# Gate/up and down products: high weights times both halves of the activations in one 512-column matmul

## What is computed

```python
hn2 = rmsnorm(x, norm2_w[l])
gu = hn2 @ w_gate_up[l]                                   # 2048 x (2 * 5632)
x = x + (jax.nn.silu(gu[..., :FFN_HIDDEN]) * gu[..., FFN_HIDDEN:]) @ w_down[l]   # 5632 x 2048
return rmsnorm(x, norm_f_w)
```

## Time and profile before

| | before |
|---|---|
| median of the runs | 2630.93 us |
| span of the profiled execution | 2631.7 us |
| its mean granted TensorE clock | 0.996 |
| TensorE matmul busy | 2584.1 us (98%) |
| VectorE busy | 1587.5 us (60%) |
| ScalarE busy | 1207.2 us (46%) |
| DMA, mean | 169 GB/s |

### The profile page before, as it was taken

How to read it: one execution, slowest core, us unless ns; L and a number is a source line. 1 busy time by engine, 2 the same in 40 slices (tenths; PEclk the granted TensorE clock), 3 DMA queues, 4 the chain that set the end, 5 groups by cost and what they waited for, 6 DMA issues and landing times.

```text
span 2631.7 us, 53153 instructions
## 1 busy us (share of the span) xinstructions
PE 2584.1 (98%) x21314; PEld 2521.6 (96%) x21314; DVE 1587.5 (60%) x1984; ACT 1207.2 (46%) x1412; POOL 44.2 (2%) x48
## 2 busy tenths in 40 slices
PE   8999999999999999999999999999999999999997
PEld 8999999999999999999999997679999999999997
DVE  6445777665455566677755556886655555555544
ACT  5444456543357665443444444234544444444442
POOL 0000021000000000000000000000000000000000
PEclk9999999999999999999999999999999999999999
DMA  6554532455554434555565653235565656555563
GB/s 226 177 175 160 176 106 80 154 186 175 178 172 157 144 111 137 186 185 193 194 205 168 207 192 120 78 99 197 185 198 192 193 191 196 191 192 194 187 199 127
DMA packets 123706, 446.06 MB, mean 169 GB/s; under 512 B 13594, under 2 KB 15925, under 8 KB 123440
## 3 DMA queue, kind: packets, MB, share of 16 engines
q1 hardware_dynamic: 122208, 438.82, 50.6%
q0 software_dynamic: 1360, 5.27, 0.6%
HBM read 441.94 MB, written 2.10 MB: 169 GB/s over the span
## 4 chain that ended last, share of the span: by engine, by line
PE 90%; DVE 5%; ACT 3%; issue 1%; DMA 0%; POOL 0%; DVEq 0%; SPq 0%; ACTq 0%
PE PS L1885 25%; PE PS L1887 25%; PE PS L1886 25%; PE PS L1948 2%; PE PS L1949 2%; PE PS L1950 2%; PE PS L2299 1%; DVE lo L1057 1%; ACT hi L540 1%; PE PS L2251 1%; PE PS L2032 0%; PE PS L2048 0%; PE PS L2131 0%; PE PS L2108 0%; PE PS L2022 0%
## 5 line engine op out<-in xcount | busy, mean ns | idle before, releaser
L1885 PE MATMUL PS<-XH,hi 128*128 128x256 f32 (+1 forms) x5152 | 1449.4, 281 | 16.7 <-DVE lo L1051 11.6
L1887 PE MATMUL PS<-XH,lo 128*128 128x256 f32 (+1 forms) x5152 | 1445.5, 281 | 0.0
L1886 PE MATMUL PS<-XL,hi 128*128 128x256 f32 (+1 forms) x5152 | 1441.0, 280 | 0.0
L1051 DVE TENSOR_TENSOR lo<-raw,hi 128x1024 fp32r<-128x1024 f32 x704 | 852.7, 1224 | 750.7 <-ACT hi L535 747.2
L535 ACT ACTIVATE hi<-raw 128x1024 fp32r<-128x1024 f32 x704 | 740.3, 1059 | 944.6 <-PE PS L1887 915.5
L1885 PEld LDWEIGHTS PS<-XH,hi 128*128 128x128 f32 x5152 | 970.2, 188 | 21.4 <-issue 16.6
L1886 PEld LDWEIGHTS PS<-XL,hi 128*128 128x128 f32 x5152 | 972.5, 189 | 1.4 <-issue 1.2
L1887 PEld LDWEIGHTS PS<-XH,lo 128*128 128x128 f32 x5152 | 969.8, 188 | 0.0
L1948 PE MATMUL PS<-XH,hi 128*128 128x256 f32 (+1 forms) x768 | 229.2, 298 | 0.3 <-DVE XL L1122 0.3
L1950 PE MATMUL PS<-XH,lo 128*128 128x256 f32 (+1 forms) x768 | 216.0, 281 | 0.0
L1949 PE MATMUL PS<-XL,hi 128*128 128x256 f32 (+1 forms) x768 | 215.8, 281 | 0.0
(11 more groups left out here) (331 smaller groups left out, 1568.3 us busy)
## 6 DMA issues: line engine op xcount, KB each, us to landing
raw<-stream SPq DMA_DIRECT2D x828, 512.0 KB, 4.1
H<-h_in SPq DMA_DIRECT2D x4, 544.0 KB, 8.2
y_win<-windows POOLq DMA_DIRECT2D x2, 1024.0 KB, 6.4
out<-H SPq DMA_DIRECT2D x4, 512.0 KB, 3.8
w_t<-w POOLq DMA_DIRECT2D x2, 512.0 KB, 5.5
dftm<-dft POOLq DMA_DIRECT2D x1, 1024.0 KB, 8.1
ml_m<-mask_ml POOLq DMA_DIRECT2D x1, 512.0 KB, 3.9
a_m<-masks_a POOLq DMA_DIRECT2D x1, 272.0 KB, 6.4
```

Source lines behind the costliest of these rows:

```text
L1051: dve.tensor_tensor(halves(lo, s, q.tokens), raw_halves(s), halves(hi, s, q.tokens).bitcast(F32), ALU.subtract)\
L1885: pe.matmul(PS[:, bank, 0:n], w_hi, x_hi, start=start, stop=False)
L1886: pe.matmul(PS[:, bank, 0:n], w_hi, x_lo, start=False, stop=False)
L1887: return pe.matmul(PS[:, bank, 0:n], w_lo, x_hi, start=False, stop=stop)
```

## The change

XH and XL become the two planes of one tensor `XHL`, and GH and GL those of `GHL`. In gate/up and down, `wide_passes` replaces `passes`: one matmul of the hi weights with a 2 x 256 column access over both planes, written to all 512 columns of the bank, and one of the lo weights with the hi plane, added to columns 0 to 255. The second half of a bank then holds w_hi*x_lo. It is added at the read-out: VectorE gets, for gate and for up, a second scaled copy out of PSUM into `g_t` and an addition; for down a second addition to `H`. ScalarE's silu waits for that addition (`g_gate`), and its final squares for both (`down_added`). The other products keep `passes`.

```diff
-        x_hi_flat = sb(ctx, "XH", [P, NT * T + 4 * STEP], F32R)
-        x_lo_flat = sb(ctx, "XL", [P, NT * T + 4 * STEP], F32R)
+        x_flat = sb(ctx, "XHL", [P, 2, NT * T + 4 * STEP], F32R)
+        x_hi_flat, x_lo_flat = x_flat[:, 0, :], x_flat[:, 1, :]
...
-            g_hi_flat = sb(ph, "GH", [P, KICK + STEP + FT * SEQ], F32R)
-            g_lo_flat = sb(ph, "GL", [P, STEP + KICK + STEP + FT * SEQ], F32R)[:, STEP:]
+            g_flat = sb(ph, "GHL", [P, 2, KICK + 2 * STEP + FT * SEQ], F32R)
+            g_hi_flat, g_lo_flat = g_flat[:, 0, :], g_flat[:, 1, :]
             g_s = sb(ph, "g_s", [P, GROUP, SEQ])
             g_p = sb(ph, "g_p", [P, GROUP, SEQ])
+            g_t = sb(ph, "g_t", [P, GROUP, SEQ])
...
+        def x_both(both, k):
+
+            at = KICK + (STEP + k * SEQ if k else 0)
+            return both[:, :, at:at + SEQ]
...
-        def bank_group(gg, n):
-            return PS[:, 4 * gg:4 * gg + GROUP, 0:n]
+        def bank_group(gg, n, at=0):
+            return PS[:, 4 * gg:4 * gg + GROUP, at:at + n]
...
             def gate_up(p, gg):
                 if gg == 0:
-                    act.wait_ge(bank_free[0], p + (q.use0[0] + 2))
+                    act.wait_ge(S("g_gate"), p + 1)
                     act.activation(g_s[:, :, :], g_s[:, :, :], ACT.Silu).then_inc(S("g_silu"), 1)
...
             def final_squares(p, gg):
-                act.wait_ge(bank_free[gg], p + (prod["down"].use0[gg] + 2))
+                act.wait_ge(S("down_added"), 2 * p + gg + 1)
                 squares(2 * p + gg, f_sq, META, SEQ)
...
-            def residual(q, gain, scratch, tok0, n):
+            def residual(q, gain, scratch, tok0, n, wide=False):
 
                 def after(p, gg):
                     group_done(dve, q, p, gg)
                     dst = H[:, p * 8 + 4 * gg:p * 8 + 4 * gg + 4, T - q.tokens:T]
+                    if wide:
+                        own(dve.tensor_tensor(dst, dst, bank_group(gg, SEQ, SEQ), ALU.add))
                     dve.tensor_tensor(dst, dst, bank_group(gg, q.tokens), ALU.add).then_inc(bank_free[gg], 1)
                     dve.wait_ge(bank_free[gg], p + (q.use0[gg] + 2))
+                    if wide:
+                        dve.sem_inc(S("down_added"), 1)
...
             def gate_up(p, gg):
                 group_done(dve, q, p, gg)
                 if gg == 0:
-                    dve.tensor_tensor(g_s[:, :, :], bank_group(0, SEQ), rs, ALU.mult).then_inc(bank_free[0], 1)
+                    dve.tensor_tensor(g_s[:, :, :], bank_group(0, SEQ), rs, ALU.mult).then_inc(S("g_scaled"), 1)
+                    dve.tensor_tensor(g_t[:, :, :], bank_group(0, SEQ, SEQ), rs, ALU.mult).then_inc(bank_free[0], 1)
+                    dve.wait_ge(S("g_scaled"), 2 * p + 1)
+                    dve.wait_ge(bank_free[0], p + (q.use0[0] + 2))
+                    dve.tensor_tensor(g_s[:, :, :], g_s[:, :, :], g_t[:, :, :], ALU.add).then_inc(S("g_gate"), 1)
                 else:
-                    dve.tensor_tensor(g_p[:, :, :], bank_group(1, SEQ), rs, ALU.mult).then_inc(bank_free[1], 1)
+                    dve.tensor_tensor(g_p[:, :, :], bank_group(1, SEQ), rs, ALU.mult).then_inc(S("g_scaled"), 1)
+                    dve.tensor_tensor(g_t[:, :, :], bank_group(1, SEQ, SEQ), rs, ALU.mult).then_inc(bank_free[1], 1)
+                    dve.wait_ge(S("g_scaled"), 2 * p + 2)
                     dve.wait_ge(bank_free[1], p + (q.use0[1] + 2))
+                    dve.tensor_tensor(g_p[:, :, :], g_p[:, :, :], g_t[:, :, :], ALU.add).then_inc(S("g_up"), 1)
+                    dve.wait_ge(S("g_up"), p + 1)
                     dve.wait_ge(S("g_silu"), p + 1)
                     dve.tensor_tensor(g_p[:, :, :], g_s[:, :, :], g_p[:, :, :], ALU.mult).then_inc(S("g_prod"), 1)
...
-            follow(dve, prod["down"], chunk, tail_gu, [(2, residual(prod["down"], "norm_f", f_xg, META, SEQ))],
+            follow(dve, prod["down"], chunk, tail_gu, [(2, residual(prod["down"], "norm_f", f_xg, META, SEQ, True))],
...
+            def wide_passes(bank, w_hi, w_lo, both, k, start, stop):
+
+                x = x_both(both, k)
+                pe.matmul(PS[:, bank, :].rearrange("p (h t) -> p h t", h=2), w_hi, x, start=start, stop=False)
+                return pe.matmul(PS[:, bank, 0:SEQ], w_lo, x[:, 0, :], start=False, stop=stop)
...
+                                    if both is None:
+                                        ins = passes(4 * gg + j, q.tokens, w_hi, w_lo, x_tile(x_hi_flat, x, q.tokens),
+                                                     x_tile(x_lo_flat, x, q.tokens), *ends)
+                                    else:
+                                        ins = wide_passes(4 * gg + j, w_hi, w_lo, both, x, *ends)
...
-            product(prod["gate_up"], between={6: lambda: squares_sum(3, g_scratch, SEQ), 7: lambda: pe.wait_ge(S("rms_ready"), 4)})
-            product(prod["down"], g_hi_flat, g_lo_flat, pieces=("gl_ready", 0, 4))
+            product(prod["gate_up"], x_flat, between={6: lambda: squares_sum(3, g_scratch, SEQ), 7: lambda: pe.wait_ge(S("rms_ready"), 4)})
+            product(prod["down"], g_flat, pieces=("gl_ready", 0, 4))
```

More of the change, by code:

```diff
@@ L1887, in passes, with product @@
                 return pe.matmul(PS[:, bank, 0:n], w_lo, x_hi, start=False, stop=stop)
-            def product(q, xh=x_hi_flat, xl=x_lo_flat, between={}, pieces=None):
+            def wide_passes(bank, w_hi, w_lo, both, k, start, stop):
+                x = x_both(both, k)
+                pe.matmul(PS[:, bank, :].rearrange("p (h t) -> p h t", h=2), w_hi, x, start=start, stop=False)
+                return pe.matmul(PS[:, bank, 0:SEQ], w_lo, x[:, 0, :], start=False, stop=stop)
+            def product(q, both=None, between={}, pieces=None):
                 def pair(p, first):
@@ L1905, in pair @@
                                     col = slice(128 * j, 128 * j + 128)
[L1906 to L1909, removed]
+                                    w_hi, w_lo = halves(hi, s, q.tokens)[:, kk, col], halves(lo, s, q.tokens)[:, kk, col]
+                                    ends = k == 0, k == 2 * q.k_chunks - 1
+                                    if both is None:
[3 more added lines that the diff above has]
+                                        ins = wide_passes(4 * gg + j, w_hi, w_lo, both, x, *ends)
                             ins.then_inc(chunk_used, 1)
```

## The result

The changed kernel takes 2668.99 us (median of four runs, 2667.98 to 2670.69), against 2630.76 for the kernel before: 1.0139 times as long, 95% interval 1.0127 to 1.0151. The forecast was 2644, the range 2619 to 2662. The sign was right; the loss of 38 us is nearly three times the one forecast.

A forecast was written before the change was run, and what follows sets the result against it. TensorE was taken to bound the kernel, with matmuls busy 98% of the span. 2631.7 + 0 for its pace + 12.1 for up read-out waits + 1.3 for the tail = 2645.1, median 2644.3 us; range 2619 to 2662.

The forecast's parts named there:

- the term for TensorE's pace: Gate/up and down: wide matmul 226.7 ns plus narrow 113.3 makes 340.0 a triple, as today; 0 us.
- The load floor: TensorE: a 128-column weight load cannot follow another in under about 112 ns; today's 113.3 sits just above.
- R3: Rival, chance 0.16: TensorE stays in its slow phase, 348 to 352 ns a triple, +17 to +25 us; 2659 to 2667.
- The up read-out: VectorE's two extra operations delay chunk 3 of the next group; TensorE waits 1.1 us at 11 places, 12.1 us.
- The tail: Behind down's last matmul: the last extra addition has nothing beside it, so the tail grows by 1.26 us.
- R1: Rival, chance 0.18: loads are free under wide matmuls; triple 329.1 or 325 ns, -23 to -32 us; median 2624 or 2617.
- R2: Rival, chance 0.17: fixed 6.7 ns price per matmul; triple 333.3 ns, -14.1 us, waits 13.8; median 2632, no change.
- R4: Rival, chance 0.07: no wait arises before chunk 3, pace unchanged; 2633.0 us, median 2632.

The follow-up runs named there:

- split: Changed kernel with the 512-column matmul done as two of 256 columns, except for each group's first input tile; 2649.35 us, 1.0059 of the kernel before.
- m_phase: Small matmul-only kernel: new and old triples in five cases of operand placement, each started 16 times behind a leading matmul of 256 to 496 columns; no whole-kernel time.
- placed: Changed kernel with gate/up and down operands at the small kernel's 340.0 ns placement, and input tile 0 in line with the others; 2652.93 us, 1.0086 of before.
- m_load: Small matmul-only kernel: 512, 416 and 256 columns with weights shortened to 128, 96, 64 and 32 columns; 512 columns took 226.7 to 233.3 ns.
- staged: Changed kernel with the up read-out cut in three, a weight conversion between the parts; 2660.43 us, 1.0107 of the kernel before.
- before_nokick: Kernel before with input tile 0 at its regular place, not 64 bytes ahead of it; 2666.25 us, single runs 2633.92 to 2670.97.
- m_sizes: Small matmul-only kernel: float32r matmuls of 64 to 512 columns, then old and new triples at displaced activations; new triple 347 to 353 ns.
- before: The kernel before the change, as profiled; 2630.76 us median.

## Why the prediction was wrong, point by point

- *The step that failed* is the term for TensorE's pace, "226.7 + 113.3 = 340.0: no change, 0 us". In the changed kernel the slots are 235 and 118, 353.3 ns together, and the term measured 25.4 us (28.2 less the group starts). `split` shows that the wide matmul brought it, `m_phase` that the new triple at this placement takes 353.3 in 16 starts of 16.
- *What the numbers of that term were.* 227 and 113 do go together: they are the slots in down of `placed`, 340.0 ns. So the sum named a pace that the new triple has, at another placement. The forecast carried nanoseconds over from rows 3 and 6 and didn't ask whether the quick pace is open to the new triple where its operands lie. Rows 6 held a warning, 16.7 ns over 173.3 at 416 columns, by the share 234 for 512, and I averaged that end away. But the share is no rule either: `m_load` has 226.7 to 233.3 ns for the same 512-column matmul, by the placement.
- *The load floor.* That "a load of 128 columns cannot follow another in less than about 112 ns" fits the 111.8 ns of 192 columns. That "today's 113.3 sits just above it" explained nothing: 256 columns beside a load of 32 take 113.3 too. And the rows of plain float32 show one of two records for each matmul (in `m_load` 24 matmuls leave 48), so 430 and 111.7 ns are prices of a record, not of "eight matmuls" or "two passes".
- *R3, the slow phase,* gave a reason, the waits (0.85 each; 9.4 us against 8.9 measured) and at its upper end the time, 2667. It had 0.16. Of its two causes `staged` rules out the interruption and `split` leaves the wide form. Its counter-argument, that "the present loop finds the quick phase again in every group", is how the slow pace came to be priced at 0: that return belongs to the old triple at this placement, with 340 among its paces (`before_nokick`, `m_phase`). It said nothing of another sequence of lengths. And the range was cut at 2662, inside the rival that rows 4 to 6 spoke for.
- *The up read-out.* Right: ready at +9.20 forecast, +9.21 measured; 11 places, none behind gate or down groups. 12.1 us became 8.9, mostly because the slower pace comes later for chunk 3 (24 x 13.3 ns = 0.32 us for each), by the rule given; the first and the last wait were shorter besides. `staged` puts them at 8.6.
- *The tail.* 1.26 as forecast for the addition, 0.7 more for sums at the lower clock. Those 0.7 had no term.
- *R1 and R2.* Both fell: the wide slot never measured under 224 ns in the changed kernel, nor a triple under 340 anywhere. The Trainium skill (TensorE: Matmul & The Clock Gate, section Back-to-back issue gap) gives N/2.4 + 2.5 ns as the gap of a single matmul by itself, and by it the triple would take 325. Plain float32 keeps the 2.5 ns over (429.2 for 426.7 a record), float32r does not.
- *R4* fell: eleven waits.

## What to carry to other kernels

Fusing two matmuls on the same weights saved nothing here: at best the fused triple kept the 340 ns of the old one, since a shorter load saved nothing, and the second half of the bank had to be read and added. Before re-cutting a tuned stream of matmuls, ask whether its pace is a steady state among several, which the trace shows by two distances between starts for one instruction; then take the slower one for the new form unless something forces the other. And count what stands ahead of the next conversion on the feeding engine: its slack, read from one read-out, gave the time at which the conversion was ready to a hundredth of a microsecond.

## What the runs showed of the hardware

- A float32r matmul of 256 or more columns went at 6.7 to 20 ns over its columns (113.3 at 256 and 233.3 at 512 in `m_sizes`). By the placement 512 columns took 226.7 to 233.3 ns, and with a load of 32 columns beside it 230.7 to 231.7 (`m_load`). On plain float32 the excess was 2.5 ns a record at 512 columns.
- Steady paces of a triple stood at 340.0, 346.7, 350.0, 353.3 and 360.0 ns, with others between (343.3, 351.1, 355.9); none was under 340. Which are open depends on the placement modulo 256 bytes, which one is taken on what ran before. For one placement the same 24 triples gave 340.0 behind 8 of 16 leading matmuls and 353.3 behind the other 8, and `before_nokick` had executions of 2634 and 2671 us. What in the chip makes the paces, the runs don't show.
- 1.99 us of idle time stood ahead of the last sums of squares in six traces. In five the granted clock over them was 0.61 to 0.78 and they took 2.47 to 3.14 us; in `placed` it was 1.00 and they took 1.99. After 0.68 us of idle time it was 1.00 (`before`, `before_nokick`).
